# The adaLN matmuls read the weights in place order, and sixteen small matmuls turn and sort the row

## The reference, cut to what matters

```
def ada_modulation(c, w_ada, b_ada):
    m = (jax.nn.silu(c) @ w_ada + b_ada)[:, None, :]
    return jnp.split(m, 6, axis=-1)
...
    sh1, sc1, gt1, sh2, sc2, gt2 = ada_modulation(c, w_ada, b_ada)
    h = rms_norm(x, g_mix) * (1.0 + sc1) + sh1
    mix, s_new, k, v, logf = token_mixer(h, ...)
    x = x + gt1 * mix
    h = rms_norm(x, g_ffn) * (1.0 + sc2) + sh2
    x = x + gt2 * moe(h, ...)
```

## Time and profile before

| | us |
|---|---|
| three runs | 949.12, 945.45, 953.24 |
| median | 949.12 |
| profiled execution | 945.33 |
| its span, first to last instruction | 943.6 |

### The profile page before, as it was taken

How to read it: one execution, slowest core, us unless ns; L and a number is a source line. 1 busy time by engine, 2 the same in 40 slices (tenths; PEclk the granted TensorE clock), 3 DMA queues, 4 the chain that set the end, 5 groups by cost and what they waited for, 6 DMA issues and landing times.

```text
span 943.6 us, 14752 instructions
## 1 busy us (share of the span) xinstructions
PE 850.4 (90%) x4815; PEld 496.7 (53%) x4816; DVE 359.8 (38%) x944; ACT 237.5 (25%) x443; POOL 36.5 (4%) x75
## 2 busy tenths in 40 slices
PE   7699999799798989999997999987999996999984
PEld 3199983526487764554543445543455443445533
DVE  2254435415413543333432333342333342233436
ACT  2343434034312321221221212221122211112224
POOL 3000011200003000000000000000000000000002
PEclk9789989689579989999998999998899998899996
DMA  9934447360062339891889498897678999998921
GB/s 329 340 129 170 179 179 278 143 235 34 1 266 108 161 144 421 330 420 71 322 335 410 184 359 354 328 357 313 257 286 335 421 417 417 419 380 365 419 117 50
DMA packets 47210, 254.41 MB, mean 270 GB/s; under 512 B 9472, under 2 KB 9808, under 8 KB 19072
## 3 DMA queue, kind: packets, MB, share of 16 engines
q1 hardware_dynamic: 39168, 247.61, 65.7%
q10 hardware_dynamic: 7200, 3.89, 1.5%
q0 software_dynamic: 736, 1.52, 0.5%
HBM read 250.34 MB, written 2.67 MB: 268 GB/s over the span
## 4 chain that ended last, share of the span: by engine, by line
PE 87%; issue 5%; DVE 4%; ACTq 2%; ACT 1%; DMA 1%; SPq 0%; DVEq 0%
PE psum L1162 24%; PE psum L1190 11%; PE psum L862 8%; PE psum L1122 8%; PE psum L1136 4%; PE psum L1043 3%; PE psum L1137 3%; PE psum L832 3%; PE psum L1129 3%; PE psum L1071 2%; PE psum L1150 2%; PE psum L1009 2%; PE psum L983 1%; PE psum L1061 1%; PE psum L995 1%
## 5 line engine op out<-in xcount | busy, mean ns | idle before, releaser
L1162 PE MATMUL psum<-expert_w,xg 128*64 128x512 f32 (+1 forms) x1184 | 224.6, 630 | 6.8 <-issue 6.8
L1590 DVE TENSOR_TENSOR acc<-psum,acc 128x288 f32<-128x288 f32 x240 | 105.0, 457 | 118.5 <-PE psum L1137 117.5
L1162 PEld LDWEIGHTS psum<-expert_w,xg 128*64 128x64 f32 (+1 forms) x1184 | 66.5, 131 | 139.7 <-issue 139.2
L1190 PE MATMUL psum<-expert_w,hidT 128*64 128x512 f32 (+1 forms) x592 | 112.1, 602 | 0.0
L1136 PE MATMUL psum<-comb,yhi 128*128 128x288 f32 x240 | 84.5, 358 | 2.7 <-DVE ylo L1613 2.5
L1122 PE MATMUL psum<-h2hl,sel 128*128 128x512 f32 x300 | 82.2, 404 | 0.5 <-ACT acc L632 0.5
L650 ACT ACTIVATE silg<-psum 128x256 f32<-128x256 f32 x29 | 11.2, 385 | 257.1 <-PE psum L1162 257.1
L1137 PE MATMUL psum<-comb,ylo 128*128 128x288 f32 x240 | 70.8, 299 | 0.0
L1122 PEld LDWEIGHTS psum<-h2hl,sel 128*128 128x128 f32 x300 | 52.4, 188 | 32.6 <-issue 17.3
L1136 PEld LDWEIGHTS psum<-comb,yhi 128*128 128x128 f32 x240 | 46.1, 192 | 33.4 <-issue 27.1
L656 ACT CAST yhi<-psum 128x1024 fp32r<-128x1024 f32 x29 | 29.4, 1012 | 117.2 <-PE psum L1190 117.2
(11 more groups left out here) (349 smaller groups left out, 998.2 us busy)
## 6 DMA issues: line engine op xcount, KB each, us to landing
expert_w<-in_w_exp_up SPq DMA_DIRECT2D x64, 1024.0 KB, 13.5
expert_w<-in_w_exp_down SPq DMA_DIRECT2D x64, 1024.0 KB, 9.4
expert_w<-in_w_exp_gate SPq DMA_DIRECT2D x64, 1024.0 KB, 11.2
ring<-in_w_ada SPq DMA_DIRECT2D x24, 1024.0 KB, 7.3
pair<-in_w_in SPq DMA_DIRECT2D x6, 2048.0 KB, 10.1
pair<-in_w_out SPq DMA_DIRECT2D x2, 2048.0 KB, 7.7
x_tok<-in_x_prompt SPq DMA_DIRECT2D x2, 512.0 KB, 4.0
cacheK<-in_cache_fox_k ACTq DMA_DIRECT2D x1, 1024.0 KB, 5.4
```

The costliest lines, as they stand in the source:

```text
L1162: last = mm(bank[3][w * x:w * x + w, :].rearrange("p (g n) -> p g n", g=2), xg[:, k, w * x:w * x + w], expert_w[:, q:q + 2, DE * k:DE * k ...
L1190: last = mm(bank[4 + half][w * x:w * x + w, :], hidT[:, i, w * x:w * x + w], expert_w[:, down_slot(g, x), o:o + 512], start=i == 0, stop=i ...
L1590: dve.tensor_tensor(acc[:, k, :], bank[6 + k % 2][:, 0:N], acc[:, k, :], ALU.add).then_inc(s["acc_ok"], 1)
```

## The change

Each of the four matmuls of `ada` reads 512 neighbouring columns of the piece. The row that comes out is in the order of the weights, so the features of one chunk are eight elements apart. `ada_T` no longer transposes four blocks. For each chunk k and each half h it makes one matmul: the stationary operand is every eighth element of `ada_row`, 128 x 64 (a step of 32 bytes), the moving one is four columns of the identity (rows 64m + 32h + g for m, g = 0, 1), and the product, 64 x 4, lands on partitions 64h to 64h + 63. These are ordinary float32 matmuls and no transposes, in two column tiles of 64. DVE reads the 32 columns that result.

```
@@ ada @@
-            cols = piece(n)[:, :].rearrange("p (m q j) -> p m j q", m=2, j=KC)
             for j in range(4):
-                last = mm(bank[b][32 * j:32 * j + 2, :].rearrange("g (j q) -> g j q", j=4), scT[:, k, :],
-                          cols[:, j // 2, 4 * (j % 2):4 * (j % 2) + 4, :], start=k == 0, stop=k == KC - 1, tile_position=(0, 32 * j))
+                last = mm(bank[b][32 * j:32 * j + 2, :], scT[:, k, :], piece(n)[:, 512 * j:512 * j + 512],
+                          start=k == 0, stop=k == KC - 1, tile_position=(0, 32 * j))
@@ ada_T @@
-            for j in range(4):
-                last = tr(bank[b][:, P * j:P * j + P], ada_row[:, P * j:P * j + P], ident[:, :])
+            rows = ident[:, :].rearrange("p (m h r) -> p h m r", m=2, h=2)
+            for k in range(KC):
+                for h in range(2):
+                    last = mm(bank[b][64 * h:64 * h + 64, 4 * k:4 * k + 4].rearrange("q (m g) -> q m g", m=2), ada_row[:, k::KC],
+                              rows[:, h, :, 0:2], start=True, stop=True, tile_position=(0, 64 * h))
@@ modulation @@
-                last = dve.tensor_tensor(adaT[:, 2 * r:2 * r + 2, g, :].rearrange("p m (h j) -> p m h j", h=2),
-                                         bank[b][:, :].rearrange("p (j m h x) -> p m h j x", j=4, m=2, h=2)[:, :, :, :, g],
-                                         b_adaT[:, 2 * r:2 * r + 2, :].rearrange("p m (h j) -> p m h j", h=2), ALU.add)
+                last = dve.tensor_tensor(adaT[:, 2 * r:2 * r + 2, g, :],
+                                         bank[b][:, 0:4 * KC].rearrange("p (k m g) -> p g m k", m=2, g=2)[:, g, :, :],
+                                         b_adaT[:, 2 * r:2 * r + 2, :], ALU.add)
```

## The result

| | before | after |
|---|---|---|
| median of the runs taken together, us | 950.02 (4 runs, 945.45 to 953.24) | 963.54 (4 runs, 960.24 to 964.41) |
| profiled execution / its span, us | 945.33 / 943.6 | 964.41 / 962.6 |
| mean granted clock of TensorE | 0.918 | 0.893 |
| first gather L1122 (after: L1124), start of the experts | 344.6 | 345.9 |
| from there to the end of the span | 599.0 | 616.7 |

The account below looks back on a forecast made before the run. The prediction took the chain of waits as the bound: ACT's queue in round 0, the stepped adaLN matmuls in rounds 1 and 2. -2.5 - 1.9 - 6.5 + 4.9 = -6.0 us, 943.1 from the median 949.12; range 935 to 951.

Parts of the forecast that it names:

- what is gained or lost before them should be passed on: Before the experts: any gain or loss reaches the end, since nothing of the change is left after they begin.
- an experts' stretch that gives the gain back: Sign that the forecast is wrong: the experts' part lengthens and cancels the gain made before it.
- the head's -6.0 us: Part before the experts: savings in rounds 1 and 2 less the sorts' extra cost, -6.0 us in all.
- The rival: Clock falls in round 1 after 3.2 us of new idle time: +3.0 us, total -3.0, 946.1 us; chance 0.20.
- Price of a matmul: adaLN matmuls: one k falls from 1.84 to 0.88 us, saving 0.95; at the low clock only some 0.2.
- Round 0 worth nothing: Round 0: PE's saving of some 6 us is hidden by waiting for ACT; zero, 3 us either way.
- Round 1: Round 1: first six k gain 2.5 us, 3.2 become PE idle time; last two k gain 1.9 us.
- Round 2: Round 2: all eight k are on the chain of waits and save 6.5 us; PE still bounds the turns.
- Sort: Small matmuls replacing the transposes, three times: 2.3 us each, 2.5 in round 0; 4.9 us more in all.
- serial rival: Sort's loads do not overlap: 4.3 us each, 949, chance 0.15; or loads and matmuls alternate: 12.5 us each, 973.6, chance 0.05.

Follow-up runs that it names:

- 176: Changed kernel with two matmuls of constants ahead of round 2's sort, experts' loop 176 instructions later than before: 959.3 us, stretch 610.5.
- 256: Changed kernel, loop 256 instructions later than before: with the filled gap 951.61 us, stretch 599.9; without it, by 88 added instructions, 951.24 us, stretch 597.2.
- 64: 16-byte-run kernel with 64 more instructions of met waits in round 0's idle time: 956.75 us, stretch 607.6.
- 0: Experts' loop not shifted: the kernel before, stretch 599.0, and the 16-byte-run kernel, 942.1 us, stretch 597.4.
- 168: Experts' loop 168 instructions later than before; the 616.7 us stretch is that of the changed kernel itself, 963.54 us.
- the filled gap: Two fp32 128x512 matmuls of constants into an unused bank ahead of round 2's transposes or sort; added to the 16-byte-run kernel: 928.94 us.
- the 16-byte-run kernel: Kernel before, its adaLN matmuls reading four neighbouring columns then stepping 32 bytes, old transposes taking every fourth column: 942.1 us, ratio 0.9953.

## Why the prediction was wrong

**The step that failed** is "what is gained or lost before them should be passed on", with "the experts' stretch unchanged". The prediction counted the sorts' instructions as time on PE and not as length of its program. That length moved the experts' loop, and the stretch took 17.7 us more. That the place does this is shown (with equal heads 10.6 us at 176 against 256, and 10.2 at 64 against 0; 597.2 at 256 against 616.7 at 168). That the waits are fetches of code is argued only: from the queue named instruction, from equal stretches 256 apart, and from the rule of the Trainium skill named above. The prediction did list "an experts' stretch that gives the gain back" among its signs of being wrong, but with no cause, price or chance.

**Also wrong: the head's -6.0 us.** It has the granted clock of round 2 unchanged, and there it fell. The rival put a fall in round 1, behind 3.2 us of idle time, at 3.0 us. In the profiled execution of after PE did idle there, and the clock stayed. But in the nine other traced kernels with fast adaLN matmuls it fell at that place. PE behind this gap in after, and in the changed kernel with the filled gap at +176:

```profile
156.55 2.67 PE L914 MATMUL psum<-ident,zt 128*128 128x128 f32 x20 [3.13 <-DVE toks L1377]
```

```profile
155.96 3.71 PE L917 MATMUL psum<-ident,zt 128*128 128x128 f32 x20 [3.14 <-DVE toks L1380]
```

There 20 transposes took 1.0 us more (0.9 to 1.6 in the nine), and the k behind them 1.62 us instead of 1.04. So the rival's place was right in nine kernels of ten, its price was some 1.6 us instead of 3.0, and the larger fall, in round 2, was not foreseen. With the clock kept, the changed kernel reaches its first gather 17.8 us earlier (330.5 against 348.3), though it does some 2 us more work. So the head ended at +1.3 us where -6.0 was forecast. This alone takes the gain away: with the place made good by 88 instructions the changed kernel took 951.24 us, some 4 of them for the added waits, where the kernel before took 948.16 beside it.

**The steps, one by one.** *Price of a matmul*: 0.442 us a pass forecast, 0.46 measured; right. At the low clock 1.82 instead of 1.94 us; right, 0.1 less than taken. *Round 0 worth nothing*: ACT's copy at 39.97 instead of 39.16; right, with 0.8 us lost and the sort on top. *Round 1*: first copy at 155.89, before 156.81, on a start 1.8 us later: 2.7 gained, 2.5 forecast. By the sort 2.0 more, 1.9 forecast. *Round 2*: from 2.95 to 9.5 us ahead, 6.6 gained though round 1's sort (2.02 for 0.44) lies in it and costs 1.6; so 8.2 against the 6.5 forecast for the eight k. Where the other 1.7 came from was not followed; the granted clock was 0.79 and 1.00 from 178 to 182 us, where before had 0.50, which may be a part of it. *Sort*: 2.02 to 2.11 us, 2.3 and 2.5 forecast; right, and neither serial rival came. The Trainium skill's price by columns alone (TensorE: Matmul & The Clock Gate, section LDWEIGHTS), 1.7 us a sort, lies between the two that were measured, 1.10 with contiguous columns and 2.02 with a step: the step decides, which its rule leaves out. (The 1.8 us by which the prediction lowers its sum there should be 2.0, since it took round 0's sort at 2.5.)

**The range** took in the clock and the loads, and no cost outside the changed stretch, so it ended at 951.

## What to carry to other kernels

Count instructions added ahead of a loop as a shift of that loop: compare PE's waits for "issue" in the untouched loop before and after, and try a few paddings before judging an edit (here 597 to 617 us for the same work). Small matmuls keep PE "busy" in the profile, and the clock can fall all the same; where a step must wait for another engine in a stretch that PE bounds, some matmuls of constants in the gap can pay (-13 us in one kernel here, none in the head of the changed kernel, where the clock fell behind the sort instead). An edit that makes PE's work lighter should be checked for the granted clock behind it, and not only for its own time.

## What the runs showed of the hardware

- The time of a loop with jumps over inner loops hangs on its place in PE's program: 597.2 to 616.7 us (up to 623.9 in executions above their kernel's median), waits of up to 10.4 us each, and equal within 2.7 us at 0 and 256.
- A moving operand of float32 with 32 bytes from element to element takes 0.918 us for a pass of four tiles of 512 columns; in place order 0.46, and runs of 16 bytes do as well as place order (647 and 642 ns a record).
- 32 loads of 64 columns with 32 small products take 1.10 us from contiguous columns and 2.02 us with a step of 32 bytes; loads and products overlap in both.
- In round 2, with no gap ahead and PE and its loads busy all the time, 2.0 us of such small products were followed within 2 us by a fall of the granted clock from 1.00 to 0.50 in three kernels. With two 512-column matmuls among them none followed in the one trace, and by the mean clock in two of four executions. In round 1 the clock fell with such a sort in three traces and did not in three others. In the kernel before it fell at 232 us with PE busy in all of the 12 us ahead.
- Idle time of 3.1 us in round 1 was followed by a fall in nine kernels and in one not. Why the kernel before kept its clock over the same gap of 1.4 us as the 16-byte-run kernel stays open; its eight k there were twice as long.
